# A third seven-product pair per gate/up chunk, and the inner tile's product moved to the fourth quad

## The chip, the cores and the metric

One Trainium2 core runs the whole program. The metric is the device time of an execution in microseconds; a kernel is given by the median of its runs.

## What is computed

Two layers of a decoder trunk on 256 tokens of width 2048, in float32: layer 0 is a pooling and gated-MLP mixer, layer 1 a Conformer convolution module. Each is followed by a dense SwiGLU feed-forward block, which is where the change is:

```
def swiglu_ffn(x, norm_pre, w_gate, w_up, w_down, norm_post):
    h = rms_norm(x, norm_pre)
    a = jax.nn.silu(jnp.einsum('bsd,df->bsf', h, w_gate)) * jnp.einsum('bsd,df->bsf', h, w_up)
    y = jnp.einsum('bsf,fd->bsd', a, w_down)
    return x + rms_norm(y, norm_post)
```

The inner width is 5632. The kernel keeps float32 accuracy by three products for each one: every operand is split into a high part (rounded to the fp32r format) and a low part (the rest), and high times high, high times low and low times high are added.

## The kernel before

**Units and quads.** All weights arrive in units of 128 x 1024 floats (512 KB), in the order in which they are used. A ring of four slots (`raw`, `w_hi`, `w_lo`) holds them; four units are a quad, numbered `q`, and unit `s` of a quad has slot `s`. For each unit the sync engine SP issues the load (line 465) once DVE has made the low part of the unit that held the slot before; ACT makes the high part `w_hi` (line 681) once the load has landed and PE has used the unit four before; DVE makes the low part `w_lo` (line 1100, or 1102 where a gain is multiplied in); PE then does 12 matmuls of 128 x 512 (line 1705): two token halves, two column halves, three passes.

**Gate/up chunks.** The inner width is cut in 11 chunks of 512 columns. A unit of chunk `i` is one 128-row tile of the input width, with 512 gate columns beside 512 up columns. A chunk has 16 units, so quads `q` to `q + 3`. Its two token halves and two column halves accumulate in four private banks of PSUM; the chunk before and this one use opposite sets.

**Pairs of seven products.** In the chunks 1 to 9 of each layer ("fast"), some pairs of neighbouring units are treated as a two-by-two block product (two token halves, two row tiles, gate and up) and done with seven products in place of eight, each product being three matmuls (`fast_pair`, lines 1895 to 1897). That needs sums of the weights, which DVE makes from the raw units before they are split (`sum_units`, lines 1347 to 1350: four operations of 128 x 512; the second replaces a part of the raw unit, so ACT waits for it with `raw_corner_ready`), ACT's high part of the three sums (line 860, 128 x 1536) and DVE's low part (line 1355). It also needs sums of the input's tiles, made once per layer (`join_rows` 1157, `sum_rows` 1164 to 1167, high part 871, low part 1172). Four of the seven products accumulate in shared banks, the private banks of the chunk before. At the chunk's end ACT copies the first (`keep_first`, 867), DVE combines them (`add_parts`, 1370 to 1373), and in the next chunk four closings (1379) add the private banks to them. Before the change the pairs are the first two units of quads 1 and 2 (`FAST_QUADS`).

**The inner tile.** After a chunk's closings, ACT's silu (845) and DVE's product (`hidden`, 1326) give 128 x 512 of the inner activation for each token half. DVE turns it in 32 x 32 blocks (`turn_hidden`, 1331), SP stores it to memory (`store_hidden`, 512) and fetches it back in another order with eight DMAs (`fetch_hidden`, 521), which completes the transposition. ACT and DVE split what came back (`hi_hid` 850, `lo_hid` 1336) into `hT_hi` and `hT_lo`.

**Down stage.** Two column halves (`j`) of 11 quads each, one quad per inner chunk. Pairs stand at quads 4 to 9 and 2 to 9. The input sums for them are made in the first four quads of `j = 0`, one batch in each: in quad 0, `join_rows` stands between DVE's splits of units 0 and 1, `sum_rows` between 1 and 2.

Each engine works through its own list, written out by hand, in order; semaphores tie them together. SP's queue is in order as well.

## Time and profile before

| | |
|---|---|
| runs | 1964.47, 1962.79, 1964.45 us; median 1964.45 |
| span of the profiled execution | 1962.1 us (no time beside its span is given) |
| PE | busy 1945.9 us, 99%, 9646 matmuls |
| DVE | busy 1570.1 us, 80% |
| ACT | busy 1114.0 us, 57% |
| DMA | 408.13 MB, mean 208 GB/s |
| granted TensorE clock | mean 0.999 |

Busy time of an engine is the union of its instructions' spans; neighbouring matmuls overlap in the records, so their pitch is read from the starts. The released-by note in brackets at a row's end gives the idle time just before it and which instruction ended it.

### The profile page before, as it was taken

How to read it: one execution, taken by the hardware profiler on the slowest of the kernel's cores; microseconds unless marked ns; L12 is line 12 of the kernel's file. 1: busy time of each engine (PE TensorE's matmuls, PEld its weight loads, DVE VectorE, ACT ScalarE, POOL GpSimd, SP SyncE). 2: the span in 40 equal slices, each digit the busy share in tenths (PEclk: the TensorE clock that was granted, in tenths of full speed). 3: DMA queues.
4: the chain of work that ended last, by engine and by line, in shares of the span. 5: the costliest groups of instructions: out<-in, count | busy, mean ns of one | idle time of the engine just before them, and what ended most of it. 6: DMA issues, size and time to landing. Idle time of an engine off the chain costs nothing.

```text
span 1962.1 us, 26334 instructions
## 1 busy us (share of the span) xinstructions
PE 1945.9 (99%) x9646; PEld 1653.3 (84%) x9646; DVE 1570.1 (80%) x2016; ACT 1114.0 (57%) x1396; POOL 201.8 (10%) x127
## 2 busy tenths in 40 slices
PE   9999999999999999999999999999999999999998
PEld 7898888888888888888899988788888888888886
DVE  5755478888888868788699996688888888688787
ACT  6544465555555545555778875465555555455454
POOL 1000000000000000000489950000000000000000
PEclk9999999999999999999999999999999999999999
DMA  9645557666766766666355545557666667766564
GB/s 330 235 144 190 182 172 236 214 229 218 241 225 223 239 222 209 211 193 207 138 193 178 184 143 194 164 195 248 225 218 212 222 228 243 241 203 214 191 213 154
DMA packets 138011, 408.13 MB, mean 208 GB/s; under 512 B 15330, under 2 KB 38498, under 8 KB 137378
## 3 DMA queue, kind: packets, MB, share of 16 engines
q1 hardware_dynamic: 135796, 396.84, 61.7%
q0 software_dynamic: 2096, 9.70, 1.3%
q8 instruction: 76, 1.25, 0.3%
q14 instruction: 43, 0.35, 0.1%
HBM read 392.84 MB, written 13.63 MB: 207 GB/s over the span
## 4 chain that ended last, share of the span: by engine, by line
PE 97%; DVE 1%; ACT 1%; issue 0%; DMA 0%; POOL 0%; SPq 0%; DVEq 0%; ACTq 0%; POOLq 0%
PE acc L1705 68%; PE acc L1896 5%; PE acc L1897 5%; PE acc L1895 5%; PE acc L1716 4%; PE acc L1718 4%; PE acc L1717 4%; DMA raw<-in_units 0%; PE acc L2057 0%; PE acc L1757 0%; DVE x L1136 0%; PE acc L1755 0%; PE acc L2035 0%; ACT junk L698 0%; DVE acc L1119 0%
## 5 line engine op out<-in xcount | busy, mean ns | idle before, releaser
L681 ACT ACTIVATE w_hi<-raw 128x1024 fp32r<-128x1024 f32 x480 | 502.3, 1058 | 488.9 <-PE acc L1705 276.8
L1100 DVE TENSOR_TENSOR w_lo<-raw,w_hi 128x1024 fp32r<-128x1024 f32 x412 | 493.8, 1219 | 147.8 <-ACT w_hi L681 146.2
L1102 DVE SCALAR_TENSOR_TENSOR w_lo<-raw,vecs,w_hi 128x1024 fp32r<-128x1024 f32 x222 | 282.6, 1282 | 161.6 <-ACT w_hi L681 161.0
L681 ACT ACTIVATE w_hi<-raw,vecs 128x1024 fp32r<-128x1024 f32 x222 | 254.7, 1152 | 250.8 <-PE acc L1705 175.2
L1705 PE MATMUL acc<-w_hi,xT_hi 128*128 128x512 f32 x1240 | 383.4, 390 | 2.3 <-DVE w_lo L1102 1.7
L1705 PE MATMUL acc<-w_lo,xT_hi 128*128 128x512 f32 x1240 | 382.0, 389 | 0.0
L1705 PE MATMUL acc<-w_hi,xT_lo 128*128 128x512 f32 x1240 | 381.8, 389 | 0.0
L1705 PEld LDWEIGHTS acc<-w_hi,xT_hi 128*128 128x128 f32 x1240 | 231.7, 188 | 52.4 <-issue 3.5
L1705 PEld LDWEIGHTS acc<-w_lo,xT_hi 128*128 128x128 f32 x1240 | 232.7, 188 | 48.6
L1705 PEld LDWEIGHTS acc<-w_hi,xT_lo 128*128 128x128 f32 x1240 | 232.7, 188 | 48.5
L1716 PE MATMUL acc<-xT_hi,w_hi 128*128 128x256 f32 x640 | 181.2, 283 | 0.0
L1718 PE MATMUL acc<-xT_hi,w_lo 128*128 128x256 f32 x640 | 181.1, 283 | 0.0
L1717 PE MATMUL acc<-xT_lo,w_hi 128*128 128x256 f32 x640 | 181.1, 283 | 0.0
L582 POOL TENSOR_TENSOR w_lo<-raw,w_hi 128x1024 fp32r<-128x1024 f32 x68 | 162.7, 2412 | 17.7 <-ACT w_hi L681 17.7
L1705 PE MATMUL acc<-w_hi,hT_hi 128*128 128x512 f32 x480 | 148.6, 389 | 0.0
L1705 PE MATMUL acc<-w_hi,hT_lo 128*128 128x512 f32 x480 | 148.5, 389 | 0.0
L1705 PE MATMUL acc<-w_lo,hT_hi 128*128 128x512 f32 x480 | 148.4, 389 | 0.0
L1716 PEld LDWEIGHTS acc<-xT_hi,w_hi 128*128 128x128 f32 x640 | 122.9, 192 | 0.0
L1717 PEld LDWEIGHTS acc<-xT_lo,w_hi 128*128 128x128 f32 x640 | 122.9, 192 | 0.0
L1718 PEld LDWEIGHTS acc<-xT_hi,w_lo 128*128 128x128 f32 x640 | 122.9, 192 | 0.0
L1558 DVE SCALAR_TENSOR_TENSOR acc<-gated,taps,acc 128x256 f32<-128x256 f32 x270 | 114.9, 480 | 1.2 <-ACT acc L979 1.2
L1705 PEld LDWEIGHTS acc<-w_hi,hT_hi 128*128 128x128 f32 x480 | 89.9, 188 | 19.2 <-issue 0.5
(276 smaller groups left out, 2697.9 us busy)
## 6 DMA issues: line engine op xcount, KB each, us to landing
raw<-in_units SPq DMA_DIRECT2D x702, 512.0 KB, 4.2
hid_turned_blocks<-tok SPq DMA_DIRECT2D x44, 256.0 KB, 4.1
tok<-hid_turned_blocks SPq DMA_DIRECT2D x176, 64.0 KB, 2.1
gpost<-in_post POOLq DMA_DIRECT2D x4, 1024.0 KB, 8.0
x<-in_x POOLq DMA_DIRECT2D x4, 512.0 KB, 8.2
c_raw<-in_consts POOLq DMA_DIRECT2D x4, 512.0 KB, 7.3
out<-x SPq DMA_DIRECT2D x8, 256.0 KB, 2.8
xT_raw<-in_xT SPq DMA_DIRECT2D x3, 512.0 KB, 7.2
```

Source lines behind the costliest of these rows:

```text
L582: nc.gpsimd.tensor_tensor(w_lo[:, s, :], raw[:, s, :], w_hi[:, s, :], ALU.subtract).then_inc(lo_ready_pool, 1)
L681: nc.scalar.activation(w_hi[:, s, :], raw[:, s, :], ACT.Copy, scale=scale).then_inc(hi_ready, 1)
L1100: ins = nc.vector.tensor_tensor(w_lo[:, s, :], raw[:, s, :], w_hi[:, s, :], ALU.subtract)
L1102: ins = nc.vector.scalar_tensor_tensor(w_lo[:, s, :], raw[:, s, :], vecs[:, gain:gain + 1], w_hi[:, s, :], ALU.mult, ALU.subtract)
L1558: nc.vector.scalar_tensor_tensor(out, gated[:, n % RING, j:j + SEQ], taps[:, n, j:j + 1], m, ALU.mult, ALU.add).then_inc(tap_done, 1)
L1705: last = mm(acc[:, 4 * par + 2 * t + h, :], xs, ws[:, s, h * BANK:(h + 1) * BANK], start=start and ws is w_hi and xs is xh, stop=stop and ...
L1716: mm(out, wh, xT_hi[:, k, :], start=start and half == 0, stop=False, skip_group_check=True)
L1717: mm(out, wh, xT_lo[:, k, :], start=False, stop=False, skip_group_check=True)
L1718: return mm(out, wl, xT_hi[:, k, :], start=False, stop=stop, skip_group_check=True)
L1895: mm(acc[:, bank, :], a_hi, b_hi, start=start, stop=False, skip_group_check=resumed)
L1896: mm(acc[:, bank, :], a_hi, b_lo, start=False, stop=False, skip_group_check=resumed)
L1897: return mm(acc[:, bank, :], a_lo, b_hi, start=False, stop=stop, skip_group_check=resumed)
```

## The change

- `FAST_QUADS = (1, 2)` becomes `FAST_AT = (4, 7, 10)`: in each fast chunk three pairs, of units 4 and 5, 7 and 8, 10 and 11, counted from the chunk's first. A pair may now lie across two quads (`next_unit`). Between them stand the plain units 6 and 9; quads 0 and 3 of a chunk stay plain.
- The input sums are made for three pairs of tiles (`gate_tiles`: tiles 8 and 9, 11 and 12, 14 and 15), in rows of 1536 columns in place of 1024. `xs_hi` and `xs_lo` grow from 2 to 3 banks each; the two banks between them and `sum_hi` were unused before, so nothing else moves.
- DVE's `hidden` of chunk `i - 1` stands in quad 3 of chunk `i` (before: quad 1), ahead of and behind the split of its unit 0; the turn stands behind the split of unit 1.
- The store stands in the queue of the next chunk, between the loads of units 1 and 2, the fetch behind unit 3's load. ACT's high part of the fetched tile stands behind its splits of units 2 and 3 of that next chunk, DVE's low part between its own splits there. For the last but one tile both stand in down's first quad: ACT's behind the four splits of that quad, DVE's behind its split of unit 0.
- `keep_first` and `add_parts` stand behind the last splits of the chunk.
- PE's wait for all but the last inner tile ahead of the down stage goes; the waits by quad stay.

Core of the diff:

```
-FAST_QUADS = (1, 2)
+FAST_AT = (4, 7, 10)

+        def gate_tiles(x):
+            return x[:, 7:KT, :].rearrange("p (a k) c -> p a (k c)", k=3)[:, :, SEQ:3 * SEQ]

 SP      def load_ffn(layer, q0):
-                for i in range(1, FFC):
-                    load_quad(i * 4 + q0, pool)
-                    load_quad(i * 4 + (q0 + 1), pool)
-                    load_quad(i * 4 + (q0 + 2), pool, (0, 1, 2))
-                    store_hidden(i - 1, layer)
-                    load_quad(i * 4 + (q0 + 2), pool, (3,))
-                    fetch_hidden(i - 1, layer)
-                    load_quad(i * 4 + (q0 + 3), pool)
+                for i in range(1, FFC + 1):
+                    q = i * 4 + q0
+                    load_quad(q, pool, (0, 1))
+                    if i >= 2:
+                        store_hidden(i - 2, layer)
+                    load_quad(q, pool, (2, 3))
+                    if i >= 2:
+                        fetch_hidden(i - 2, layer)
+                    load_quad(q + 1, pool)
+                    if i < FFC:
+                        load_quad(q + 2, pool)
+                        load_quad(q + 3, pool)

 ACT     for i in range(1, FFC):
-                    split_quad(i * 4 + q0, gain, 0)
+                    q = i * 4 + q0
+                    for s in range(4):
+                        split(q, s, gain + s)
+                        if i >= 2 and s >= 2:
+                            hi_hid(i - 2, s - 2)
                     silu(i - 1, 0)
                     silu(i - 1, 1)
+                    u = 4
+                    while u < 12:
+                        if i in FAST_CHUNKS and u in FAST_AT:
+                            split_pair(q + u // 4, u % 4, gate_sum(layer, i, FAST_AT.index(u)), gate_raw_sum)
+                            u += 2
                         else:
+                            split(q + u // 4, u % 4)
+                            u += 1
+                    split_quad(q + 3, gain, 4)
+                    if i in FAST_CHUNKS:
+                        keep_first(gate_sum(layer, i, len(FAST_AT) - 1), par if i % 2 == 0 else 1 - par, parts, i)
...
                             split_quad(q)
                         if j == 0 and c == 0:
+                            hi_hid(FFC - 2, 0)
+                            hi_hid(FFC - 2, 1)
                             silu(FFC - 1, 0)
                             silu(FFC - 1, 1)

 DVE
                     for s in range(3):
                         split(q, s, gain + s)
+                    if i >= 2:
+                        lo_hid(i - 2, 0)
                     if i - 1 in FAST_CHUNKS:
                         (two closings)
                     split(q, 3, gain + 3)
+                    if i >= 2:
+                        lo_hid(i - 2, 1)
...
+                    while u < 12:
+                        if fast and u in FAST_AT:
+                            n = FAST_AT.index(u)
+                            if n:
+                                sum_units(q + u // 4, u % 4, gate_sum(layer, i, n), gate_raw_sum)
+                            split_pair(q + u // 4, u % 4, gate_sum(layer, i, n), gate_raw_sum, gate_sum_lo[:])
+                            u += 2
+                        else:
+                            split(q + u // 4, u % 4)
+                            u += 1
+                    split(q + 3, 0, gain + 4)
                     if i - 1 in FAST_CHUNKS:
                         dve.wait_ge(closed, closed_count(layer, i - 1))
                         hidden(i - 1, 0)
                         hidden(i - 1, 1)
-                    split(q + 1, 2)
+                    split(q + 3, 1, gain + 5)
                     turn_hidden(i - 1, 0)
                     turn_hidden(i - 1, 1)
...
                     split(q + 3, 2, gain + 6)
                     split(q + 3, 3, gain + 7)
+                    if fast:
+                        add_parts(gate_sum(layer, i, len(FAST_AT) - 1), closing(layer, i - 1), z, parts)
...
                             split(q, 0)
+                            if c == 0:
+                                lo_hid(FFC - 2, 0)
+                                lo_hid(FFC - 2, 1)
                             if c:
                                 lo_batch(c - 1)

 PE
+                    while u < 12:
+                        k = u + 4
+                        if i in FAST_CHUNKS and u in FAST_AT:
+                            n = FAST_AT.index(u)
+                            pe.wait_ge(rows_lo_ready, rows + 1)
+                            fast_pair(q + u // 4, u % 4, gate_sum(layer, i, n), z, xT_hi, xT_lo, k, ...)
+                            u += 2
                         else:
+                            plain_units(q + u // 4, (u % 4,), xT_hi, xT_lo, k - u % 4, z)
+                            u += 1
+                    quad(q + 3, xT_hi, xT_lo, 4, z, stop=gu0_ready)
                 qd = q0 + Q_FF
-                pe.wait_ge(hT_lo_ready, 22 * layer + 20)
```

## Rows read from the trace of the kernel before

**Rows 1.** The page: the span, the chain by engine, the costliest PE group.

```profile
span 1962.1 us, 26334 instructions
...
PE 97%; DVE 1%; ACT 1%; issue 0%; DMA 0%; POOL 0%; SPq 0%; DVEq 0%; ACTq 0%; POOLq 0%
...
L1705 PE MATMUL acc<-w_hi,xT_hi 128*128 128x512 f32 x1240 | 383.4, 390 | 2.3 <-DVE w_lo L1102 1.7
```

**Rows 2.** Windows (stretch, length, busy per engine, granted clock, DMA share, GB/s).

```profile
463.00:505.00 42.00, 42.00 (x187) 34.79 (x186) 36.32 (x41) 23.13 (x23) 0.00 (x0) 1.00 0.66 221
...
14.00:16.00 2.00, 1.14 (x5) 0.99 (x6) 2.00 (x3) 1.68 (x2) 0.00 (x0) 1.00 0.67 254
```

**Rows 3.** PE timeline (start, length): first matmuls of one chunk's two pairs.

```profile
474.72 0.39 PE L1895 MATMUL acc<-w_hi,xT_hi 128*128 128x512 f32 x1
...
484.92 0.39 PE L1895 MATMUL acc<-w_hi,xT_hi 128*128 128x512 f32 x1
```

**Rows 4.** DVE timeline of two fast chunks in layer 0.

```profile
445.76 1.29 DVE L1336 TENSOR_TENSOR hT_lo<-tok,hT_hi 128x512 fp32r<-128x512 f32 x2
...
450.71 0.68 DVE L1370 TENSOR_TENSOR parts<-acc,parts 128x512 f32<-128x512 f32 x1
...
465.28 1.28 DVE L1102 SCALAR_TENSOR_TENSOR w_lo<-raw,vecs,w_hi 128x1024 fp32r<-128x1024 f32 x1 [0.24 <-ACT w_hi L681]
466.49 0.68 DVE L1347 TENSOR_TENSOR gpost<-raw 128x512 f32<-128x512 f32 x1
...
469.14 1.28 DVE L1379 TENSOR_TENSOR parts<-acc,parts 128x512 f32<-128x512 f32 x2
470.34 2.35 DVE L1100 TENSOR_TENSOR w_lo<-raw,w_hi 128x1024 fp32r<-128x1024 f32 x2
472.61 1.75 DVE L1355 TENSOR_TENSOR gate_sum_lo<-gpost,sum_hi 128x1536 fp32r<-128x1536 f32 x1
474.28 1.41 DVE L1326 SCALAR_TENSOR_TENSOR tok<-parts,x_rs,tok 128x512 f32<-128x512 f32 x2
475.61 1.22 DVE L1100 TENSOR_TENSOR w_lo<-raw,w_hi 128x1024 fp32r<-128x1024 f32 x1
476.74 1.29 DVE L1331 STREAM_TRANSPOSE tok<-tok 128x512 f32<-128x512 f32 x2
```

**Rows 5.** ACT timeline of the same stretch.

```profile
443.98 1.13 ACT L850 ACTIVATE hT_hi<-tok 128x512 fp32r<-128x512 f32 x2
...
467.93 1.06 ACT L681 ACTIVATE w_hi<-raw 128x1024 fp32r<-128x1024 f32 x1 [1.45 <-DVE raw L1348]
...
470.50 1.47 ACT L860 ACTIVATE sum_hi<-gpost 128x1536 fp32r<-128x1536 f32 x1
```

**Rows 6.** SP's fetches; loads' landing times (line 465, layer 0's chunks); the page's store row.

```profile
482.06 4.81 SPq L521 DMA_DIRECT2D tok<-hid_turned_blocks  x8
...
DMA to landing us min/median/max: 3.1/4.2/8.5
...
hid_turned_blocks<-tok SPq DMA_DIRECT2D x44, 256.0 KB, 4.1
```

**Rows 7.** Timeline at layer 0's entry into the down stage: PE, ACT, DVE.

```profile
718.16 0.61 PE L1705 MATMUL acc<-w_hi,hT_hi 128*128 128x512 f32 x2
...
718.42 1.06 ACT L681 ACTIVATE w_hi<-raw 128x1024 fp32r<-128x1024 f32 x1 [1.66 <-PE acc L1705]
...
715.21 0.42 DVE L1164 TENSOR_TENSOR down_raw_sum<-down_raw_sum 128x256 f32<-128x256 f32 x1
```

**Rows 8.** Timeline of each layer's first fast chunk: DVE's low sums, PE's products.

```profile
306.23 1.75 DVE L1355 TENSOR_TENSOR gate_sum_lo<-gpost,sum_hi 128x1536 fp32r<-128x1536 f32 x1
...
308.80 0.39 PE L1895 MATMUL acc<-sum_hi,xs_hi 128*128 128x512 f32 x1
...
1311.54 1.75 DVE L1355 TENSOR_TENSOR gate_sum_lo<-gpost,sum_hi 128x1536 fp32r<-128x1536 f32 x1
...
1312.26 0.39 PE L1895 MATMUL acc<-w_hi,xT_hi 128*128 128x512 f32 x1
```

More of the change, by code:

```diff
@@ L898, in ffn @@
                         if c in FAST_DOWN[j]:
-                            split_fast(q, down_sum(layer, j, c), down_raw_sum[:])
+                            split_pair(q, 0, down_sum(layer, j, c), down_raw_sum[:])
+                            split(q, 2)
+                            split(q, 3)
                         elif c == FFC - 1:
@@ L1409, in ffn @@
                             close(kept, 1 - z, parts, t, 1)
[L1410 to L1413 removed]
+                    u = 4
+                    while u < 12:
[9 more added lines that the diff above has]
+                    split(q + 3, 0, gain + 4)
                     if i - 1 in FAST_CHUNKS:
```

115 lines of the change are left out of this document (38 added, 77 removed).

## The prediction

> **What bounds the kernel now.** I read the page first: the span and the chain that ended last, 97% of it PE in a span of 1962.1 us [rows 1]. The profiled execution has no time of its own beside the span; the median of the runs, 1964.45, lies 2.35 us above it, and I carry that 2.35 over. So a matmul taken off PE is worth its whole pitch, as long as the weights go on arriving in time. The window over one gate/up chunk [rows 2] says how tight that is: in 42.00 us PE is busy throughout at a granted clock of 1.00, DVE for 36.32, ACT for 23.13. DVE is the engine to watch. The matmul pitch comes from PE's timeline [rows 3]: the first matmuls of two pairs of one chunk are 484.92 - 474.72 = 10.20 us apart, with 21 + 24 = 45 matmuls between: 0.2267 us each. So a plain unit (12 matmuls) is 2.72 us, a pair (21) is 4.76, a chunk with two pairs (186) 42.16, one with three (183) 41.48.
>
> **What is removed.** Nine fast chunks in each of two layers gain a third pair. Each pair has 21 matmuls where two plain units have 24: 18 x 3 x 0.2267 = 12.2 us less PE time. Everything below asks how much of this the other engines take back.
>
> **What DVE must now do in a chunk.** Durations are start-to-start differences in its timeline [rows 4]. A split with gain 1.21 (465.28 to 466.49), a plain split 2.27 / 2 = 1.135 (470.34 to 472.61), the four sums of a pair 2.65 (466.49 to 469.14), two closings 1.20, the low part of the sums 1.67 (472.61 to 474.28), hidden 1.33 (474.28 to 475.61), the turns 1.29 busy as a pair, so about 1.22. add_parts is four operations of the same size as the sums: 2.65. The two low splits of the fetched tile show 1.29 busy as a pair, so 1.20 pitch. Per chunk: 8 x 1.21 + 8 x 1.135 + 3 x 2.65 + 3 x 1.67 + 2 x 1.20 + 1.33 + 1.22 + 1.20 + 2.65 = 40.5 us, against 41.48 of PE. One more pair costs DVE 4.32 and takes 0.68 from PE. The slack falls from some 6 us to 1.0, yet DVE does not become the longer one. In the fast zone DVE is even slower than PE: pair plus unit is 3 x 1.135 + 2.65 + 1.67 = 7.73 against 4.76 + 2.72 = 7.48, so it loses 0.25 twice and must live on its lead.
>
> **The lead.** Put 0 where PE starts unit 0 of a steady chunk. ACT may split a unit once PE has left the one four before; in the rows its start follows that end by 0.26 (718.42 for a unit ended at 718.16 [rows 7]). So ACT splits unit 2 at -2.46, DVE follows at -1.28, then one fetched split, two closings, unit 3, the other fetched split: sum of units 4 and 5 from 3.54. Sums 2.65, closings 1.20, two splits 2.27, low sums 1.67: done at 11.4; PE wants them at 10.88 + 2.72 = 13.6, lead 2.2. Unit 6, then pair 7-8: low sums done 19.1, wanted 21.1, lead 2.0. Unit 9, pair 10-11: done 26.9, wanted 28.6, lead 1.7. ACT keeps pace: its first split of a pair waits for the second DVE sum (467.93, 1.4 after the first sum starts), and its copy of the sums runs 470.50 to 471.97 [rows 5], in a pair without closings just as DVE reaches its low part. Then unit 12, hidden, 13, turns, 14, 15, add_parts: done at 37.0, where the next chunk's PE start wants the parts at 41.48. Unit 0 to unit 2 of the next chunk: DVE reaches unit 2 at 39.4 and waits for ACT until 40.2. The schedule closes on itself with 0.8 us idle. Between the lower bound (PE never waits) and the upper (DVE's 40.5 plus every wait DVE now has at ACT, above 42.16 if more than 1.7 us of such waits stay) I take the lower, since the rows of a two-pair chunk show DVE without idle from 465.28 to the turns.
>
> **The moved step.** The turned tile's store now stands between the loads of units 1 and 2 of the next chunk, its fetch after unit 3's load. The queue issues in order, so what stands behind the fetch is the load of units 4 and 5, which the first pair's sums wait for. Store at about 32; its landing takes 4.1 [rows 6] so 36; eight fetch issues take up to 4.81 (the slowest of those I read [rows 6]): free at 39.7 to 41, where the queue before would have loaded unit 4 at 38.3 (DVE's low split of unit 0). Unit 5's data then stand about 4.2 later (median of the loads; 3.1 when alone, 8.5 at worst): 44 to 45.5, which is 2.5 to 4.0 in the new chunk, against 3.54 for the sums. At most 0.5 late with these, and the lead of 1.7 swallows it. Cost 0; if a landing near 8.5 falls there, a stall of up to 3 us, once; for such chances I book 0.3 in all. At the other end of the chunk, the pause that the fetch made before unit 12 is gone; nobody on PE waited there, so no gain.
>
> **The first fast chunk.** Three row sums in place of two: join, high and low rows from 1024 to 1536 columns (1.22 to 1.75 by the rows of those widths [rows 4]) and four small operations from 256 to 384 (0.42 [rows 7], against 0.68 at 512: 0.55). On DVE's path ahead of the first sums this is about 0.5 for the join, 0.5 for the small ones, 0.5 for the low rows, part of it in waits that existed. In layer 0 the low sums end at 306.23 + 1.75 = 307.98 and PE begins the products that wait for them at 308.80 [rows 8]: lead 0.8, of which about 0.7 goes; then the fast zone loses 0.25 twice. That is short by 0.4 us at the last pair. Bounds 0 and 1.5 (all additions uncovered). In layer 1 they end at 1311.54 + 1.75 = 1313.29 and are wanted 2.72 after the pair's start at 1312.26 [rows 8], so at 1314.98: lead 1.7, cost 0.
>
> **The entry into down.** This is the large term. The last but one tile's fetched split, formerly in the third quad of the chunk, now stands in down's first quad: ACT does it after all four splits of that quad, DVE between its splits 0 and 1. ACT's fourth split waits for PE to leave the last gate/up unit: 718.42, right after PE ended it at 718.16 [rows 7]. So DVE stands behind its split 0 until the engine order lets it go on, with split 1 behind it: ACT is free at 718.42 + 0.96 = 719.38, first high part done 720.01, second 720.5 (1.13 for two [rows 5]), DVE's two low parts to 721.3, the join that also stands ahead of split 1 until 722.4 (pitch 1.11 to 1.15), split 1 done 723.6. PE wants unit 1 at 718.16 + 2.72 = 720.88. It stands 2.7 us, plus some 0.15 to get going. Behind, the row sums (four at 0.42 busy [rows 7], 1.7 in all) and split 2: done 726.4, 0.1 late. hidden, split 0, low rows, turns, join and split 1 of the second quad run back to back and come out level with PE (0.1 to 0.2). Together 3.1 us a layer, 6.2 in all; before, every one of these was done early. Bounds: 2.5 (no ripple) to 4.5 (the second quad's row sums late as well) a layer.
>
> **Sum:** -12.2 + 6.2 + 0.4 + 0.3 = -5.3: span 1956.8, and 1964.45 - 5.3 = 1959.1.
>
> **The clock.** PE's longest wait for weights before is 1.7 us [rows 1], in the stretch 14 to 16, where the granted clock stays 1.00 [rows 2]. The new wait is 2.7, longer than any in this trace. The Trainium skill, TensorE: Matmul & The Clock Gate, Part 1 (The HAM clock gate), says that an array left idle falls to half rate and needs sustained work to come back; no row here shows it at that length. By that rule the sum would be dearer, which is rival C.
>
> **Rivals.**
> A. The gate/up chunks lose time (the other side). Place: the wait of DVE's first sums for unit 5 behind the fetch, or any DVE wait inside the fast zone. With 1.0 us slack a chunk, DVE cannot make good more than that; lateness beyond it carries into the next chunk and becomes PE idle. If each chunk loses 1.0 beyond slack and lead, that is 16 x 1.0 = 16 us, and the time is 1959 + 16 = 1975. It decides from 0.33 a chunk (5.3 / 16). For it: 40.5 of 41.48, loads that took 8.5. Against: the leads of 1.7 to 2.2 and a down stage where pairs already recur every 10.2 us with DVE at 4 x 1.135 + 2.65 + 1.67 = 8.9. Chance 0.13.
> B. The down stall is hidden (full gain): 1964.45 - 12.2 + 0.4 = 1952.7. It needs ACT's fetched split to come ahead of its fourth split; the order in the code speaks against it. Chance 0.07.
> C. The stall happens and PE comes back at 1.2 GHz. Each unit at half rate costs another 2.72: one per layer gives 1959.1 + 5.4 = 1964.5, a whole quad 1959.1 + 21.8 = 1981. Against: 1.7 us without effect. Chance 0.07.
> D. Small stalls in gate/up, 0.1 to 0.3 a chunk, or a longer ripple in down: 1961 to 1964. Chance 0.15.
> E. The change does not do what it says (a pair falls out): the row counts would show it. Below 0.01.
> Forecast 0.58, with its own range 1956.5 to 1961.
>
> **Range and chances.** 1953.5 to 1964.5 leaves out most of A and B and the dear end of C, about 0.2. A measurement of this kernel can tell about 0.2%, 3.9 us, from no change: faster is below 1960.5, slower above 1968.4. Faster: most of the forecast (0.54) + B 0.07 + a little of D 0.04 = 0.65. Slower: A 0.10, C 0.02 = 0.12. Same: 0.23.
>
> **What would show it.** Matmuls of the product lines 54 x 7 more in products and 18 x 24 fewer in units. A steady gate/up chunk 41.5 us long with PE idle 0 and DVE busy about 40.6. PE idle, released by DVE's plain split, of 2.6 to 3.1 us 2.7 us after the down stage begins in both layers, with ACT's tile split right behind the fourth w_hi split. A few tenths in layer 0's first fast chunk. It is wrong if PE shows idle in most chunks (A), none in down (B), or the granted clock below 1.00 after the stall (C).

## The result and the profile after

The changed kernel takes 1986.68 us (median of 4 runs, 1983.77 to 1988.24) against 1964.46 in the same comparison (1962.79 to 1964.88): ratio 1.0116, 95% interval 1.0104 to 1.0129. It is 22 us slower, where 5.3 us faster was predicted. The page of its profiled execution (columns as in [rows 1]; the group of plain unit matmuls, L1705 before, is L1721 now):

```profile
span 1984.1 us, 26388 instructions
...
PE 60%; DVE 24%; DMA 10%; issue 3%; ACT 2%; SPq 1%; POOL 0%; DVEq 0%; ACTq 0%; POOLq 0%
...
L1721 PE MATMUL acc<-w_hi,xT_hi 128*128 128x512 f32 x1096 | 339.4, 391 | 0.6 <-DVE xT_lo L1159 0.6
...
hid_turned_blocks<-tok SPq DMA_DIRECT2D x44, 256.0 KB, 5.5
```

The chain was 97% PE; now 24% of it is DVE and 10% transfers. 1240 - 1096 = 144 matmuls of each of three kinds are gone, the 432 of 18 x 24; the pairs brought 18 x 21 = 378, and 9646 - 9592 = 54 are saved. PE's own waits (what waited for what: us in total, times, longest):

```profile
PE acc L1911 <- DVE w_lo L1113: 11.5, 12, 2.0
PE acc L1721 <- DVE w_lo L1113: 5.5, 2, 2.7
```

The first are the pairs of the gate/up chunks, the second the two entries into down. Where the pairs of one chunk start, and the first pair of the next (PE's timeline):

```profile
606.67 0.47 PE L1911 MATMUL acc<-w_hi,xT_hi 128*128 128x512 f32 x1 [0.20 <-DVE w_lo L1113]
...
648.79 0.47 PE L1911 MATMUL acc<-w_hi,xT_hi 128*128 128x512 f32 x1
656.53 0.47 PE L1911 MATMUL acc<-w_hi,xT_hi 128*128 128x512 f32 x1
664.26 0.47 PE L1911 MATMUL acc<-w_hi,xT_hi 128*128 128x512 f32 x1
```

7.74 and 7.73 from pair to pair, which is not PE's 7.48 but DVE's 3 x 1.135 + 2.65 + 1.67 = 7.73; and 648.79 - 606.67 = 42.12 for a chunk that should take 41.48. Others take up to 44.0; from the first pair of layer 0's first fast chunk to that of its ninth the mean is 343.43 / 8 = 42.93, where a chunk with only two pairs took 42.16. A gap shows in PE's waits only at the first product of some pairs (0.20 here): the rest hides between matmuls, so busy time says 100% of PE and only the pitch tells. The windows, as [rows 2]:

```profile
631.00:673.00 42.00, 42.00 (x184) 33.83 (x183) 40.24 (x46) 22.80 (x24) 0.58 (x1) 1.00 0.73 237
...
1748.00:1750.00 2.00, 2.00 (x6) 1.56 (x6) 1.93 (x5) 0.98 (x2) 0.00 (x0) 0.53 0.76 260
1750.00:1752.00 2.00, 2.00 (x7) 1.52 (x7) 2.00 (x4) 1.05 (x3) 0.00 (x0) 0.61 0.46 123
1752.00:1754.00 2.00, 2.00 (x11) 1.65 (x10) 2.00 (x3) 1.03 (x1) 0.00 (x0) 1.00 0.74 213
```

The granted clock was also low for a while between the two layers, where the kernel before had 1.00 in the same work:

```profile
1157.00:1159.00 2.00, 2.00 (x9) 1.68 (x9) 1.90 (x6) 2.00 (x6) 2.00 (x2) 0.66 0.50 150
1159.00:1161.00 2.00, 2.00 (x6) 1.56 (x5) 2.00 (x6) 2.00 (x7) 2.00 (x1) 0.50 0.78 211
```

In the first window DVE is busy for 40.24 of 42.00. What makes it wait in the chunks of layer 0 (295 to 720):

```profile
DVE w_lo L1115 <- ACT w_hi L691: 13.1, 14, 1.7
DVE hT_lo L1349 <- ACT hT_hi L860: 8.3, 9, 1.2
DVE w_lo L1113 <- ACT w_hi L691: 7.5, 6, 2.0
DVE gpost L1361 <- DMA raw<-in_units: 4.6, 6, 1.5
```

Inside the chunks that is some 2.5 us each, where the slack was 1.0. In all 16 steady chunks (those that follow the first fast one, both layers) DVE waits for the fetched tile's high part, 0.5 to 1.3 us, in sum 14.0; for a load ahead of the first sums it waits in 7 of them, in sum 3.5. The third piece is the entry into down (PE's timeline, first of layer 0, then of layer 1):

```profile
729.18 0.73 PE L1721 MATMUL acc<-w_hi,hT_hi 128*128 128x512 f32 x2 [2.73 <-DVE w_lo L1113]
...
1747.27 0.73 PE L1721 MATMUL acc<-w_hi,hT_hi 128*128 128x512 f32 x2 [2.73 <-DVE w_lo L1113]
```

**The ledger of the spans:** -12.2 for the matmuls. +24.2 in the gate/up chunks: from the first to the last pair of a layer 358.9 us where the hand schedule has 346.8, so 12.1, twice; 1.4 and 1.8 of that arise in each layer's first fast chunk, the other 21.0 in the steady ones. +3.4 in layer 0's down stage: from its first matmul to its first pair 48.19 us (723.56 to 771.75) where the kernel before took 44.88. +4.6 in layer 1's (49.50, 1741.66 to 1791.16): the same stall, and 1.3 by the half clock behind it. +1.7 between the layers, by the half clock at 1158. +0.1 and +0.9 in the last chunks, -0.7 ahead of layer 0. Together 22.0, as 1984.1 - 1962.1.

### The profile page after: what moved, and what is told of

The parts are those of the page before. It is cut to its first block, busy times and chain, and to the rows that moved or that the text cites. A ratio compares the mean times of both kernels' runs of the same rounds, so it can differ in the third digit from the quotient of the medians.

```text
span 1984.1 us, 26388 instructions
## 1 busy us (share of the span) xinstructions
PE 1951.8 (98%) x9592; PEld 1640.5 (83%) x9592; DVE 1642.9 (83%) x2106; ACT 1127.7 (57%) x1414; POOL 202.4 (10%) x127
## 4 chain that ended last, share of the span: by engine, by line
PE 60%; DVE 24%; DMA 10%; issue 3%; ACT 2%; SPq 1%; POOL 0%; DVEq 0%; ACTq 0%; POOLq 0%
PE acc L1721 38%; DVE w_lo L1113 6%; DMA raw<-in_units 4%; DMA hid_turned_blocks<-tok 4%; PE acc L1732 4%; PE acc L1734 4%; PE acc L1733 4%; DVE gate_sum_lo L1369 3%; PE acc L1911 3%; PE acc L1912 3%; PE acc L1913 3%; DVE w_lo L1115 3%; DMA tok<-hid_turned_blocks 2%; DVE gpost L1361 2%; DVE gpost L1364 2%
## 5 line engine op out<-in xcount | busy, mean ns | idle before, releaser
L1721 PE MATMUL acc<-w_hi,xT_hi 128*128 128x512 f32 x1096 | 339.4, 391 | 0.6 <-DVE xT_lo L1159 0.6
L1721 PE MATMUL acc<-w_lo,xT_hi 128*128 128x512 f32 x1096 | 337.6, 389 | 0.0
L1721 PE MATMUL acc<-w_hi,xT_lo 128*128 128x512 f32 x1096 | 337.5, 389 | 0.0
L1721 PEld LDWEIGHTS acc<-w_hi,xT_hi 128*128 128x128 f32 x1096 | 204.5, 188 | 46.0 <-issue 2.3
L1721 PEld LDWEIGHTS acc<-w_lo,xT_hi 128*128 128x128 f32 x1096 | 205.8, 188 | 42.9
L1721 PEld LDWEIGHTS acc<-w_hi,xT_lo 128*128 128x128 f32 x1096 | 205.8, 188 | 42.9
L1721 PE MATMUL acc<-w_hi,hT_hi 128*128 128x512 f32 x480 | 149.6, 391 | 5.5 <-DVE w_lo L1113 5.5
L1721 PE MATMUL acc<-w_hi,hT_lo 128*128 128x512 f32 x480 | 149.2, 391 | 0.0
L1721 PE MATMUL acc<-w_lo,hT_hi 128*128 128x512 f32 x480 | 149.0, 390 | 0.0
L1721 PEld LDWEIGHTS acc<-w_hi,hT_hi 128*128 128x128 f32 x480 | 89.9, 188 | 26.0 <-DVE w_lo L1113 7.0
```

What stands on the lines that cost most here:

```text
L1721: last = mm(acc[:, 4 * par + 2 * t + h, :], xs, ws[:, s, h * BANK:(h + 1) * BANK], start=start and ws is w_hi and xs is xh, stop=stop and ...
```

## The experiments

The theories. **S:** the chunks lose time to the moved store and fetch, which leave DVE more to wait for than its slack. Within it, **Q:** it is the eight issues of the fetch, which hold SP's queue and the loads behind them; **B:** it is the bytes, which crowd the loads and land late themselves. The rival to S, **V:** DVE has too much work, and any three-pair chunk runs at its pace. A chunk's length is taken from its first pair to the next chunk's first pair.

**The entry into down.** The low part of the last but one tile goes where DVE has time, behind unit 2's split.

```diff
-                            if c == 0:
-                                lo_hid(FFC - 2, 0)
-                                lo_hid(FFC - 2, 1)
...
-                            if c == 0:
-                                dve.wait_ge(hT_lo_ready, 22 * layer + 20)
+                            if c in (0, 2):
+                                dve.wait_ge(hT_lo_ready, 22 * layer + 18 + c)
...
-                            if c == 3:
+                            if c in (0, 3):
```

> The changed kernel with one thing moved: DVE's low part of the last but one tile stands behind its split of unit 2 of down's first quad, not behind the split of unit 0, so that nothing that waits for PE stands ahead of units 1 and 2. Theory (the stall at down's entry is this order alone): the two waits of 2.73 us go, and with them the half clock behind the one in layer 1; 1986.7 - 5.5 - 3 = about 1978. Rival (DVE reaches down late in any case and the wait only moves to the next quad): within 1 us of 1986.7.

1973.45 us, ratio 1.0054 (1.0037 to 1.0071). Both waits at L1721 and the half clock behind the second are gone. The median fell by 13.2 us, but the repair itself is worth 8.0: by the profiled executions the two down stages are 3.3 and 4.7 shorter. The rest is none of its doing: the low clock between the layers did not occur (1.7), and the stretch ahead of layer 0, layer 0's chunks and layer 1's last chunk were shorter by 1.0, 1.2 and 0.7. The chunks stay long (10.9 and 12.0 lost, where it was 12.1 twice). This repair is called e1 below.

**Two pairs, all else as changed.**

```diff
-FAST_AT = (4, 7, 10)
+FAST_AT = (4, 8)
```

> The changed kernel with two pairs a chunk again, at units 4 and 8, and all else as changed. Theory S (a saturated DVE: with three pairs it has 40.5 us of work in 41.5, so each wait for a late load or fetch, some 2.5 us a chunk, lengthens the chunk): with two pairs DVE has 36.2 and the same waits vanish in its slack; chunks of 42.16, first pair to last pair without PE idle; 1964.5 + 6.2 at down's entry + up to 4 of clock = 1971 to 1975. Rival M (the moved store, fetch and inner tile delay PE by themselves): chunks stay near 42.9 or above, time 1983 or more.

1972.36 us, 1.0047 (1.0031 to 1.0064), inside what was expected. Each chunk takes exactly 42.16 and PE waits nowhere in them, with the same store and fetch in the same places: with 6 us of slack they cost nothing. What is left against the kernel before is the two entries into down (4.6 and 4.7, both with the half clock).

**Store and fetch as small transfers, three pairs.** Only one partition of the tile is stored and 512 bytes fetched per issue, so the output lacks most of the hidden tiles.

```diff
-sp.dma_start(d_hid[t], tok[:, t * DA + BANK:(t + 1) * DA])
+sp.dma_start(d_hid[t][0:1, :], tok[0:1, t * DA + BANK:(t + 1) * DA])
...
-    sp.dma_start(dst, src[quadrant])
+    sp.dma_start(dst[0:1, 0:1], src[quadrant][0:1, 0:1])
```

> The changed kernel, in which the inner tile's store and fetches carry one partition each (2 KB and 512 bytes in place of 256 and 64 KB), with the same semaphores and places; the output is not the reference's. Theory S, with the transfers as the source of the waits: the loads of units 1 to 3 land in 3 to 4.5 us in place of 7 to 8 at worst, chunks fall from 42.9 to 41.5-41.8, time 1986.7 - 18 to 22 = 1965 to 1969 (less some clock). Rival D (DVE's own work and its semaphores fill 42.9 us whatever arrives): chunks stay at 42.9, time 1984 or more.

1963.52 us, 0.9996 (0.9987 to 1.0006). Behind the first fast chunks 12 of 14 take the steps 7.48, 7.48 and 26.52, in sum 41.48 (the two others 41.50 and 41.71). The window over one of them:

```profile
628.34:669.82 41.48, 41.48 (x185) 34.35 (x183) 40.34 (x47) 24.13 (x24) 0.58 (x1) 1.00 0.67 227
```

DVE's work of 40.3 to 40.5 does fit in 41.48, and V falls. Of the 23 us that came off, 20.6 are in the gate/up chunks: they are S.

**The third pair alone**, with the inner tile, its store, its fetch and `add_parts` where they were before.

```diff
-                    load_quad(q, pool, (0, 1))
-                    if i >= 2:
-                        store_hidden(i - 2, layer)
...
+                    load_quad(i * 4 + (q0 + 2), pool, (0, 1, 2))
+                    store_hidden(i - 1, layer)
+                    load_quad(i * 4 + (q0 + 2), pool, (3,))
+                    fetch_hidden(i - 1, layer)
```

> The third pair alone: pairs at 4, 7, 10, but the inner tile's product, turn, store, fetch and splits, and the closing steps, in the places they had before (product and turn in the second quad, splits of the fetched tile ahead of unit 12). Theory S: DVE's work between units 4 and 12 grows to 3 x 7.73 + 3.8 + 1.2 = 28 us against 19.7 of PE, and in quads 3 and 0 it can not run ahead by more than the ring; chunks of 44 to 46, time 1964.5 - 12.2 + 17 x 3.5 = about 2010. Rival M (what costs is the move of the inner tile): no down stall, 1952 to 1965.

1980.49 us, 1.0086 (1.0069 to 1.0102). Neither the 2010 expected nor the rival's 1952 to 1965, and no stall at down, but its chunks take 42.0 to 44.1 behind the first as well, and 13.3 and 13.2 us are lost a layer: the old place of the step holds a three-pair chunk up as much as the new one. So the move is not the culprit by itself; store and fetch cost about as much beside three pairs in either place.

**Only the fetch small** (the output lacks the tiles).

```diff
-    sp.dma_start(dst, src[quadrant])
+    sp.dma_start(dst[0:1, 0:1], src[quadrant][0:1, 0:1])
```

> The changed kernel with the store at full size (2 x 256 KB) and each fetch cut to 512 bytes; the output is not the reference's. With store and fetch both small the chunks fell from 42.9 to 41.48 and the time to 1963.5. If it is the store amid the loads of units 1 to 3 (loads of 7 to 8 us beside it), the waits for those loads stay, and only DVE's wait for the fetched tile shrinks: chunks 42.2 to 42.6, time 1972 to 1980. If it is the fetch, chunks 41.5 and 1963 to 1966.

1962.41 us, 0.9998 (0.9988 to 1.0008), chunks 41.48 to 41.96 behind the first, with the store whole. It is the fetch. But its issues became shorter along with its bytes (2.3 to 2.6 us for eight instead of 3.65 to 4.8), so Q and B are both alive. Two more runs part them.

**Sixteen issues of 512 bytes** hold SP longer than the whole fetch (4.66 us as the median of its 22 fetches, where the changed kernel has 3.65), without its bytes (the output lacks the tiles).

```diff
-                        sp.dma_start(dst, src[quadrant]).then_inc(hid_fetched[t], 16)
+                        for k in range(2):
+                            sp.dma_start(dst[0:1, k:k + 1], src[quadrant][0:1, k:k + 1]).then_inc(hid_fetched[t], 16)
```

> The changed kernel with the fetch of 512 bytes as in the run with a small fetch, but issued as sixteen transfers instead of eight, so that SP is held as long as by the full fetch (8 issues took 2.3 to 2.6 us there, so 16 about 4.6 to 5.2; the full fetch takes 3.65 to 4.8) while almost no bytes move. Theory Q (the fetch costs because its issues hold SP's queue and the loads of units 4 and 5 behind it come late): the loss is back, steady chunks 42.5 to 43, 1976 to 1988 us. Theory B (the fetch costs by its bytes: its own late landing, awaited by ACT and DVE, and the crowding of the neighbours): steady chunks stay near 41.5 to 41.8 and the time at 1961 to 1966. The fetched tile's data are mostly not moved, so the output is not the reference's.

1986.07 us, 1.0113 (1.0096 to 1.0130): a loss of the whole size is back without the bytes. 14.6 and 13.8 us are lost in the layers' chunks, more than the changed kernel's 12.1.

**One plain copy of 256 KB per token half**, two issues with all the bytes (the tile arrives in another order, so the output differs).

```diff
-                    for quadrant in range(4):
-                        dst = tok[32 * quadrant:32 * (quadrant + 1), ...]
-                        sp.dma_start(dst, src[quadrant]).then_inc(hid_fetched[t], 16)
+                    sp.dma_start(tok[:, t * DA:t * DA + BANK], d_hid[t]).then_inc(hid_fetched[t], 16)
```

> The changed kernel with the store as it is and the fetch as one plain copy of 256 KB per token half, two issues instead of eight, all bytes moved. Theory Q: SP is held for some 1 us, the loads of units 4 and 5 leave as early as in the run with a small fetch, 1961 to 1968 us. Theory B: the bytes still crowd the loads, 1975 to 1986. Both may hold a part: then the time lies between. The tile arrives in another layout, so the output is not the reference's.

1966.64 us, 1.0011 (1.0001 to 1.0020): 20 of the 22 us gone, with all bytes moved; 3.4 and 3.7 are lost in the layers' chunks, 1.5 and 1.7 of them in the first. So Q holds in the main. SP's timeline of a chunk shows it, first of the changed kernel, then of the sixteen issues, of the small fetch, and of the two issues (start, length, times):

```profile
629.16 0.92 SPq L520 DMA_DIRECT2D hid_turned_blocks<-tok  x2
630.92 1.53 SPq L473 DMA_DIRECT2D raw<-in_units  x2
634.20 3.65 SPq L529 DMA_DIRECT2D tok<-hid_turned_blocks  x8
637.89 12.24 SPq L473 DMA_DIRECT2D raw<-in_units  x6
```

```profile
637.03 4.65 SPq L530 DMA_DIRECT2D tok<-hid_turned_blocks  x16
641.72 18.94 SPq L473 DMA_DIRECT2D raw<-in_units  x9
```

```profile
624.84 2.30 SPq L529 DMA_DIRECT2D tok<-hid_turned_blocks  x8
627.18 33.12 SPq L473 DMA_DIRECT2D raw<-in_units  x14
```

```profile
626.58 0.97 SPq L526 DMA_DIRECT2D tok<-hid_turned_blocks  x2
628.04 32.38 SPq L473 DMA_DIRECT2D raw<-in_units  x13
```

And the first two pairs that follow in the last three, again PE's timeline (the changed kernel's stand above, at 648.79 and 656.53):

```profile
651.59 0.47 PE L1912 MATMUL acc<-w_hi,xT_hi 128*128 128x512 f32 x1
...
659.32 0.47 PE L1912 MATMUL acc<-w_hi,xT_hi 128*128 128x512 f32 x1
```

```profile
639.57 0.39 PE L1911 MATMUL acc<-w_hi,xT_hi 128*128 128x512 f32 x1
...
647.05 0.39 PE L1911 MATMUL acc<-w_hi,xT_hi 128*128 128x512 f32 x1
```

```profile
641.23 0.39 PE L1908 MATMUL acc<-w_hi,xT_hi 128*128 128x512 f32 x1
...
648.71 0.39 PE L1908 MATMUL acc<-w_hi,xT_hi 128*128 128x512 f32 x1
```

The chunk begins on PE 10.88 before its first pair. The load of unit 4 goes out, relative to that start, at 641.72 - 640.71 = +1.0 with sixteen issues, 637.89 - 637.91 = 0.0 in the changed kernel, -1.5 with the small fetch and -2.3 with two issues; the first two run their pairs at 7.73, the last two at 7.48. Over all 16 steady chunks the order is the same: that load leaves later with eight whole or sixteen small issues (-0.7 to +2.2, counted from PE's first matmul of the chunk) than with the small fetch or two issues (-3.4 to -0.4).

**What sixteen issues do not copy.** They hold SP 1.0 us longer, and the loss goes another way. There DVE waits for a load ahead of the first sums in all 16 steady chunks, 23.3 us in sum, and for the tile 3.1; in the changed kernel it was 3.5 and 14.0. Half of the tile stands behind four issues (1.75 us) and lands about 2.9 after the last of them; with one plain issue per half it stood behind 0.33 and landed about 3.4 after it, and the waits for it fell to 2.5. So the length of the issues delays both the tile and the loads, and DVE waits for whichever is later in its list. That the issues alone would cost just 21 us at the real length of 3.65 is not shown.

**Light add_parts** (e1 with the four operations of L1382 to L1385 a quarter as wide in most chunks, so the output is off): DVE has some 1.5 us less to do a chunk (1643.1 - 1618.7 over 16 chunks), at the end of it.

```diff
-                    q6, q7, q5 = [acc[:, shared_bank(z, i), :] for i in (1, 2, 3)]
+                        q6, q7, q5 = [acc[:, shared_bank(z, i), 0:P] for i in (1, 2, 3)]
```

> As e1_down_entry (1973.5) with add_parts a quarter as wide in the chunks 2 to 9 of gate/up: some 1.3 to 1.6 us of DVE work less a chunk, outside the loop from turn to first sums; the output is not the reference's. Slack theory (DVE's 40.5 of 41.5 plus 2.5 of waits): chunks shorter by the whole of it, 1973.5 - 10 or more = 1963 or less. Loop theory (turn to sums 14.3, sums to turn 28.3, together 42.6): DVE merely waits longer, 1971 to 1974.

1970.75 us, 1.0036 (1.0022 to 1.0049), 2.7 less than e1, with intervals that overlap. DVE's idle time in 340 to 690 grows from 21.9 to 32.2 us, some 1.3 a chunk, nearly all that was taken off. That too speaks against V. That a shorter DVE would help more between the fetch's end and the turn is a guess from the order of the lists; no run shows it.

**Attempts to make room, all on e1.** Each of these was expected between 1955 and 1963 us, and none came there. The low part of the fetched tile on POOL:

```diff
-                    nc.vector.tensor_tensor(by_token(hT_lo, i, t), fetched(t), by_token(hT_hi, i, t),
+                nc.gpsimd.tensor_tensor(by_token(hT_lo, i, t), fetched(t), by_token(hT_hi, i, t),
```

> As e1_down_entry, but the low part of the fetched tile is made by POOL in place of DVE: 1.2 us of DVE's work less in a chunk and no wait of DVE for the fetch (some 1 us a chunk); stores, fetches and loads stay where they crowd. Theory S (what decides is DVE's slack against its waits): slack 2.2 in place of 1.0, waits 1.5 in place of 2.5: chunks 41.5 to 41.9, time 1973.5 - 10 to 15 = 1958 to 1963. Rival P (the late loads hold PE back whatever DVE's slack is, or POOL's access slows DVE): 1969 or more.

1971.25 us, 1.0039 (1.0025 to 1.0053). In layer 0's chunks (295 to 720) e1's waits of DVE for that tile, 9.8 us, are gone, and its waits for raw units (the sums) rose from 3.2 to 14.2: the loads behind the fetch, as Q has it. Store and fetch apart, behind the loads of units 3 and 5, the tile's split later:

```diff
-                    load_quad(q, pool, (0, 1))
+                    load_quad(q, pool)
                     if i >= 2:
                         store_hidden(i - 2, layer)
...
+                    load_quad(q + 1, pool, (0, 1))
                     if i >= 2:
                         fetch_hidden(i - 2, layer)
```

> As e1_down_entry, with the store behind unit 3's load and the fetch behind the load of unit 5, the fetched tile's splits behind ACT's silu and DVE's last closings. Same work on DVE; the store stands in the pause while DVE does add_parts. Theory S with crowding: loads of units 1 to 3 land in 3 to 5 us, no DVE wait for the fetch, chunks 41.5 to 41.8; time 1964.5 - 12.2 + 2.8 for the two first chunks + up to 4 = 1955 to 1959, below both kernels. Rival (any place of the transfers costs the same in a DVE with 1 us slack): within 3 us of 1973.

1985.32 us, 1.0095 (1.0074 to 1.0116): the waits for raw units are 22.1 us, where e1 has 3.2; by the order of the queue, loads inside the fast zone (of units 6 and 7) now stand behind the fetch. Both edits together gave 1980.54, 1.0079 (1.0058 to 1.0100), where 1955 to 1956 was expected. From POOL's queue:

```diff
-                sp.dma_start(dst, src[quadrant]).then_inc(hid_fetched[t], 16)
+                pool.dma_start(dst, src[quadrant]).then_inc(hid_fetched[t], 16)
```

> As e1_down_entry (1973.5), with the inner tile's store and fetches issued from POOL's queue, which is idle here; sizes unchanged. What is asked: small fetches alone gave 1962.4, and the wait left behind e6 was the first pair's sums waiting for unit 5, whose load stood behind 4.4 us of fetch issues. Theory Q (the queue: store's landing plus eight fetch issues hold the loads of units 4 and 5): SP's loads now go out right after DVE's low parts, unit 5 has landed in time, chunks 41.5 to 41.8, time 1955 to 1959. Rival T (the transfers themselves: 512-byte packets beside the loads slow them whoever issues them): DVE's waits for raw stay at 10 us or more in all, chunks 42.3 or above, time 1967 or more.

2108.0 us, 1.0736 (1.0718 to 1.0754). One tile's two stores and eight fetches took from 431.85 to 450.10. POOL's timeline, and one row of DVE's:

```profile
431.85 1.13 POOL L616 DMA_DIRECT2D hid_turned_blocks<-tok  x2 [32.37 <-DVE tok L1346]
436.69 1.68 POOL L624 DMA_DIRECT2D tok<-hid_turned_blocks  x3 [3.72 <-DMA hid_turned_blocks<-tok]
442.17 1.64 POOL L624 DMA_DIRECT2D tok<-hid_turned_blocks  x3 [3.79 <-issue]
447.02 0.55 POOL L624 DMA_DIRECT2D tok<-hid_turned_blocks  x1 [3.21 <-issue]
449.55 0.55 POOL L624 DMA_DIRECT2D tok<-hid_turned_blocks  x1 [1.99 <-issue]
...
447.39 0.69 DVE L1351 TENSOR_TENSOR hT_lo<-tok,hT_hi 128x512 fp32r<-128x512 f32 x1 [5.99 <-ACT hT_hi L862]
```

Between the fetches stand 2.0 to 3.8 us in which POOL waits for nothing shown. This says nothing of Q. The pieces moved to the store (four per half) and a fetch of two issues:

```diff
-                sp.dma_start(d_hid[t], tok[:, t * DA + BANK:(t + 1) * DA]).then_inc(hid_stored[t], 16)
+                for quadrant in range(4):
+                    sp.dma_start(dst[quadrant], src).then_inc(hid_stored[t], 16)
...
+                sp.dma_start(tok[:, t * DA:t * DA + BANK], d_hid[t]).then_inc(hid_fetched[t], 16)
```

> As e1_down_entry, but the reordering is done by the store (four issues of 64 KB a token half, 512-byte pieces) and the fetch is one plain copy of 256 KB a half. So two issues stand ahead of units 4 and 5 in place of eight. Theory Q: SP is free some 3 us earlier, the tile is back earlier too; chunks 41.5 to 41.9, 1955 to 1961. Rival T: the same bytes beside the same loads, waits stay: 1967 or more.

1971.56 us, 1.0045 (1.0028 to 1.0062). SP holds 3.69 us for the store now, ahead of unit 2's load, and DVE's waits moved there: for high parts of gain splits they are 18.0 us in layer 0's chunks where e1 has 12.5, for the tile 1.4 where it has 9.8. The same transfers from ACT's queue:

```diff
-                sp.dma_start(dst[quadrant], src).then_inc(hid_stored[t], 16)
+                act.dma_start(dst[quadrant], src).then_inc(hid_stored[t], 16)
```

> As e10_one_fetch (store in four 64 KB pieces a half, fetch in one), but issued from ACT's queue: the stores after keep_first, the fetch between ACT's splits of units 1 and 2, the fetched tile's splits after silu and the last closings. SP carries loads alone. Loop theory: unit 5's load leaves the loop, chunks 41.5 to 41.8, 1955 to 1959. If the transfers themselves crowd the loads: DVE's waits for raw stay, 1965 or more. If ACT's issues cost it more than about 0.5 us each, its splits of units 0 and 2 come late: above 1970.

1985.4 us, 1.0108 (1.0091 to 1.0125): ACT issues them between its splits, and DVE waits 23.7 us for high parts of gain splits (340 to 690). Last, hidden and turn ahead of unit 12's split, so that the store starts earlier:

```diff
+                    hidden(i - 1, 0)
+                    hidden(i - 1, 1)
+                    turn_hidden(i - 1, 0)
+                    turn_hidden(i - 1, 1)
                     split(q + 3, 0, gain + 4)
```

> As e1_down_entry, with hidden and the turn ahead of unit 12's split in place of around it and unit 13's, and the store ahead of the load of the next chunk's unit 0. DVE's work is the same; the loop is shorter by the two splits, 2.4 us: 42.6 - 2.4 = 40.2, below PE's 41.48. Loop theory: chunks 41.5 to 41.9, the steady waits gone, up to 0.3 a chunk at unit 12: 1955 to 1962, below before. Slack theory: nothing changes but the place, 1971 or more.

1977.19 us, 1.0062 (1.0042 to 1.0081). The fast zone runs at 7.48 in most chunks, but unit 12 is now late: PE waited 14.9 us in 15 waits for gain splits. Its split had been done 1.0 ahead of PE in e1, and hidden and turns take 2.55.

**Three pairs in every second chunk.** If the loss is of slack, a two-pair chunk between makes it good. Third pairs in the odd fast chunks, or in the even ones, both on e1:

```diff
+PAIRS_AT = {i: FAST_AT[:2 + i % 2] for i in FAST_CHUNKS}
+PAIRS_AT = {i: FAST_AT[:2 + (i in (2, 4, 6, 8))] for i in FAST_CHUNKS}
...
-                        if i in FAST_CHUNKS and u in FAST_AT:
+                        if i in FAST_CHUNKS and u in PAIRS_AT[i]:
```

> The repaired down entry (run e1), and a third pair only in the odd chunks 1, 3, 5, 7, 9; the even ones have pairs at units 4 and 7 alone. If a chunk with three pairs loses only because DVE's 1.0 us slack does not cover the fetch's 2.5 us a chunk, a chunk with two (slack some 6) in between restores the lead: an odd and an even chunk together take 41.48 + 42.16 = 83.64 plus at most 0.5. The two-pair run took 1972.36 with both down stalls; without these 13.2 less (as between the changed kernel and e1), 1959.2; ten third pairs at 0.68 less give 1952.4; half of the gain lost 1956. So 1952 to 1959, faster than before (1964.5). If the loss arises inside each three-pair chunk (the late loads of units 4 and 5 stall PE whatever the lead), each odd chunk takes about 43 and the time is 1960 to 1967.

> As the run with odd chunks, but the third pair in chunks 2, 4, 6 and 8, so that the first fast chunk, which came late by 1.2 to 1.8 us in the changed kernel, and the last have two pairs only. Eight third pairs instead of ten: 1.4 us more by matmuls, up to 3.0 less by the first chunks' lateness. 1952 to 1959, within 2 us of the odd version; against it 1960 to 1967 if the loss is inside each three-pair chunk.

Odd: 1962.22 us, 0.9994 (0.9985 to 1.0003). Even: 1960.19 us, 0.9983 (0.9974 to 0.9992), against 1963.84 in the same comparison: the only version tried that is faster than the kernel before, by 3.7 us. Both lie above the 1952 to 1959 expected and inside the time that the rival gave, yet not by the rival's mechanism: in the even version two-pair chunks take 42.16 and three-pair chunks 41.48, but for two in layer 0 (42.38 and 41.71). In the odd version, whose first fast chunk has three pairs, this holds from the fifth on; the four before are 0.4 to 2.2 longer, and 3.7 and 2.1 us are lost in the two layers. The expectations were too low because they took 13.2 us off the two-pair run for its down entries, which by its own trace cost 9.3. From a chunk's first pair to the next chunk's (PE's timeline, even version, a three-pair chunk):

```profile
599.06 0.39 PE L1910 MATMUL acc<-w_hi,xT_hi 128*128 128x512 f32 x1
...
640.77 0.47 PE L1910 MATMUL acc<-w_hi,xT_hi 128*128 128x512 f32 x1
```

41.71 here, the longest of the eight. SP held 4.46 us for the fetch ahead of the next chunk's load of unit 4, at 629.85, that is 0.04 ahead of its chunk (10.88 before 640.77), as late as in the changed kernel; that chunk has two pairs and bears it.

## Why the prediction was wrong

**The failed step is "Cost 0" for the moved step**, and with it the 0.3 booked for chances; measured, 21.0 in the steady chunks. Several of its single figures were close. SP was to be free at 39.7 to 41 of a chunk of 41.48; in the chunk shown it was free at 637.85, 0.06 ahead of the next chunk's start at 637.91, which is 41.4 on that count. The sums of units 4 and 5 were to start at 3.54; DVE's timeline of the changed kernel:

```profile
637.64 1.28 DVE L1115 SCALAR_TENSOR_TENSOR w_lo<-raw,vecs,w_hi 128x1024 fp32r<-128x1024 f32 x1 [0.51 <-ACT w_hi L691]
639.77 0.69 DVE L1349 TENSOR_TENSOR hT_lo<-tok,hT_hi 128x512 fp32r<-128x512 f32 x1 [0.85 <-ACT hT_hi L860]
...
643.57 0.69 DVE L1361 TENSOR_TENSOR gpost<-raw 128x512 f32<-128x512 f32 x1
```

643.57 - 637.91 = 5.66, late by 2.1. ACT's rows say why: its split of unit 2 waited for a load issued behind the store, and the fetched tile's first half landed at 639.1.

```profile
636.45 1.15 ACT L691 ACTIVATE w_hi<-raw,vecs 128x1024 fp32r<-128x1024 f32 x1 [1.72 <-DMA raw<-in_units]
639.11 0.63 ACT L860 ACTIVATE hT_hi<-tok 128x512 fp32r<-128x512 f32 x1 [1.51 <-DMA tok<-hid_turned_blocks]
```

**A wait that the sum put at nothing.** The prediction asks only what the fetch does to the loads behind it. It never sets the fetched tile's own landing against its first reader, though ACT's high part stands right behind the split of unit 2, which was to start at -2.46, and DVE's low part right behind DVE's. In the steady chunks the first half landed 0.1 to 1.4 behind 0 (10.88 ahead of the first pair), and DVE waited for it in every one, 14.0 us in sum. In the chunk shown only 0.11 of waiting, for a load, stood between that wait and the late sums; the rest was DVE's own work.

**Lead and slack.** The reasoning also failed in what was done with a lateness. I set "at most 0.5 late" against a lead of 1.7 and called it swallowed. But a lead is spent once and a chunk recurs nine times a layer; what renews it is the slack, 1.0 us. Once the lead is gone, PE goes at DVE's 7.73 through the pairs and every further wait of DVE is PE's. The runs with two pairs, in every chunk or in every second one, show the slack's part in it. By the order of the lists these waits should also feed themselves (a late turn makes a late store, a late fetch, late loads, and so a late turn in the next chunk); no run takes this apart from the rest. The store's landing was also longer than the 4.1 of [rows 6]: 5.5 as the page's median. That comes with the new place and not with the lack of slack, for the two-pair run with 6 us of slack has 5.4.

**Matmuls, -12.2:** right. **DVE's 40.5 in 41.48:** right (40.34 in the 41.48 of the run with small transfers), and the schedule written out by hand is right as well: in that run nearly every chunk takes 41.48, with the first sums at 3.52 where 3.54 was predicted.

**The first fast chunk:** 0.4 and 0 predicted for the last pair; PE's and DVE's timelines of the changed kernel have

```profile
321.76 0.47 PE L1911 MATMUL acc<-w_hi,xT_hi 128*128 128x512 f32 x1 [1.08 <-DVE w_lo L1113]
...
1339.39 0.47 PE L1911 MATMUL acc<-w_hi,xT_hi 128*128 128x512 f32 x1 [1.59 <-DVE w_lo L1113]
```

```profile
317.74 0.69 DVE L1361 TENSOR_TENSOR gpost<-raw 128x512 f32<-128x512 f32 x1 [1.02 <-DMA raw<-in_units]
...
1335.36 0.69 DVE L1361 TENSOR_TENSOR gpost<-raw 128x512 f32<-128x512 f32 x1 [1.73 <-DMA raw<-in_units]
```

Against PE's pitch from the layer's first pair, the last pairs are 1.44 and 1.75 late (layer 0's first stands at 305.36, layer 1's at 1322.68; by pitch the last one follows 14.96 later). DVE waited for a load ahead of that pair's sums, 1.02 and 1.73, which my sum did not hold; layer 1's is above the upper bound of 1.5 that the text gave for layer 0.

**The entry into down:** place and cause right, size of the wait right (2.73 against 2.7 both times), 3.4 in layer 0 against 3.1. In layer 1 the granted clock fell to 0.53 and 0.61 after PE had come back, and the entry cost 4.6. That is rival C, at 0.07, in one layer of two, at 1.3 us instead of the 2.7 it gave a layer. The low clock between the layers, another 1.7, stands in no term.

**The clock.** A wait of 2.73 in layer 0 of the changed kernel left it at 1.00 (730 to 736); the same wait with small transfers did not (windows as above, 718 to 724 of that run):

```profile
718.00:720.00 2.00, 1.05 (x5) 0.87 (x6) 1.93 (x4) 0.00 (x0) 0.00 (x0) 1.00 0.16 16
720.00:722.00 2.00, 2.00 (x7) 1.57 (x6) 1.97 (x4) 1.30 (x2) 0.00 (x0) 0.56 0.71 246
722.00:724.00 2.00, 2.00 (x7) 1.56 (x6) 2.00 (x3) 1.25 (x2) 0.00 (x0) 0.58 0.59 199
```

So the same wait may or may not bring the 1.2 GHz level for up to 4 us, and it comes after the wait, while PE works. By the Trainium skill, TensorE: Matmul & The Clock Gate, Part 1 (The HAM clock gate), the gate judges the recent busyness on a schedule of its own; the traces agree in that equal waits ended differently. Its price at this place is 0 or about 1.3 us a wait: with the low clock the entries cost 4.6 to 4.7 in the changed kernel, the two-pair run and the run with small transfers, without it 3.3 to 3.4 in the changed kernel and the run with the small fetch.

**Rival A was what happened, by its mechanism** (lateness beyond the slack, carried from chunk to chunk and paid by PE), at 10.5 us a layer in the steady chunks instead of 8. The place that it named first, DVE's first sums waiting for unit 5 behind the fetch, was the smaller part: 3.5 us in 7 of 16 chunks, against 14.0 for the tile itself. It had 0.13. The rows for a larger chance were there: 40.5 of 41.48, a landing of 8.5, and eight issues of up to 4.81 us ahead of the loads. I let the median of landings that were taken with 6 us of slack stand for those with 1.

**What stays open:** whether the landing times of the loads (median 4.3, up to 8.4) and of the tile add to Q's cost; two issues with all bytes leave 3 to 4 us between 1966.64 and the two runs with a small fetch, about the size of that run's scatter (1962.4 to 1969.0). A fetch of the right order in two issues was not tried, nor one in eight plain pieces, so what the 512-byte pieces cost beside their issues is not shown. Nor is it shown why the clock fell between the layers.

## What to carry to other kernels

A lead is a stock and slack is a flow: a lateness that recurs in every turn of a loop is to be set against the slack of one turn, not against the lead. Where an engine is booked to 98%, price each issue that a queue makes ahead of its loads, by its own row, and count issues before bytes: here the same bytes in two issues a chunk in place of eight took 20 us off. Set every transfer's landing against its own first reader too, and not only against what stands behind it in the queue. And where a saving leaves no slack, try it in every second turn: 3.7 us of gain were kept so, and lost when taken everywhere.

## What the runs showed of the hardware

- The issue of a transfer on SP took 0.46 us in pieces of 64 KB (eight in 3.65, at times 4.8), 0.29 with 512 bytes (sixteen in 4.65, eight in 2.30), 0.46 to 0.49 for a plain 256 KB (two in 0.92 to 0.97). From 64 to 256 KB it hardly grew.
- The same ten transfers from POOL's queue took 18.3 us, 3.7 of them a wait for the store's landing; from SP's they took 0.92 and 3.65 beside that wait. By the Trainium skill, SBUF — State Buffer, SBUF: two separate sides, GpSimd cannot write the descriptors of its transfers while DVE runs an operation in a mode that takes the port they share. The trace does not bear that out as the cause here: of POOL's gaps marked "issue", the one of 3.21 us (443.81 to 447.02) lies wholly in the 5.99 us in which DVE was idle (to 447.39). What fills them stays open.
- PE's busy share does not show a late feed: with pairs 7.73 apart instead of 7.48 it reads 42.00 of 42.00.
- In the changed kernel the granted clock was 0.50 in 1496 to 1498, behind a wait of PE of 1.92 us that ended at 1494.6, and 0.53 in 1748 to 1750, behind one of 2.73 that ended at 1747.3; behind one of 2.73 that ended at 729.2 it stayed at 1.00.
